# First step of a fused transformer block: x and weight loads take turns, and the first modulation product ends a step later

## The reference, cut to what matters

```python
# first block, first lines (l = 0)
x = x + 0.5 * swiglu(rms_norm(x, ffn1_norm[l]), ffn1_w_gate[l], ffn1_w_up[l], ffn1_w_down[l])
# swiglu(h, w_gate, w_up, w_down) = (silu(h @ w_gate) * (h @ w_up)) @ w_down
...
# second block: six vectors of 1024 out of one row c
c_act = silu(c)
mod = (c_act @ w_mod[l] + b_mod[l])[:, None, :]
```

## Time and profile before

| | |
|---|---|
| median of three executions | 1753.6 us (1753.0 to 1753.9) |
| profiled execution, own time | 1755.12 us |
| its span in the profile | 1753.2 us |
| PE busy | 1736.8 us, 99% |
| DVE, ACT, POOL busy | 1063.4, 738.9 and 197.1 us |
| the chain that ended last | PE 93%, DVE 3%, DMA 2%, ACT 1% |
| granted clock of PE, mean | 0.998 |

### The profile page before, as it was taken

The page is one execution under the profiler, slowest core; times in us unless marked ns, Lnnn a source line. Parts: engine busy times, 40 slices in busy tenths (PEclk is TensorE's granted clock), DMA queues, the critical chain, the costliest instruction groups (busy, mean ns, idle before and its releaser), DMA issues.

```text
span 1753.2 us, 23718 instructions
## 1 busy us (share of the span) xinstructions
PE 1736.8 (99%) x8898; PEld 1424.7 (81%) x8898; DVE 1063.4 (61%) x1649; ACT 738.9 (42%) x1043; POOL 197.1 (11%) x245
## 2 busy tenths in 40 slices
PE   8999999999999999999999999999999999999998
PEld 7888888888888777788888888888987888888887
DVE  6666537555563767655788853437588565555433
ACT  5322222333444887623333222225575455555321
POOL 2222001130000000004511020120004200000000
PEclk9999999999999999999999999999999999999999
DMA  7777422342222212123755552325132233222232
GB/s 246 249 226 226 138 75 81 107 151 96 97 73 96 73 49 69 55 94 111 220 180 157 147 169 81 99 90 187 47 144 73 73 104 98 99 98 83 81 102 78
DMA packets 171714, 206.87 MB, mean 118 GB/s; under 512 B 18420, under 2 KB 150130, under 8 KB 171122
## 3 DMA queue, kind: packets, MB, share of 16 engines
q1 hardware_dynamic: 145010, 161.97, 28.7%
q0 software_dynamic: 12640, 38.55, 7.0%
q10 hardware_dynamic: 13984, 5.27, 1.4%
HBM read 190.29 MB, written 17.56 MB: 119 GB/s over the span
## 4 chain that ended last, share of the span: by engine, by line
PE 93%; DVE 3%; DMA 2%; ACT 1%; issue 1%; SPq 0%; POOL 0%; DVEq 0%
PE bank L2270 40%; PE bank L2197 35%; PE bank L2548 5%; PE bank L2572 1%; PE bank L2669 1%; DMA w_raw<-in_w_in 1%; PE bank L2165 1%; PE bank L2288 1%; PE bank L2582 1%; PE bank L2923 1%; PE bank L2442 1%; PE bank L2935 1%; DMA w_raw<-in_ffn_w_gate 1%; PE bank L2791 0%; DMA mod_raw<-in_w_mod 0%
## 5 line engine op out<-in xcount | busy, mean ns | idle before, releaser
L737 ACT CAST w_hi<-w_raw 128x2048 fp32r<-128x2048 f32 x156 | 298.1, 1911 | 726.2 <-PE bank L2270 354.8
L1306 DVE TENSOR_TENSOR w_lo<-w_raw,w_hi 128x2048 fp32r<-128x2048 f32 x158 | 369.3, 2337 | 343.1 <-ACT w_hi L737 342.5
L2270 PE MATMUL bank<-h_hi,w_hi 128*128 128x512 f32 x1024 | 400.8, 391 | 0.5 <-DVE h_lo L1347 0.2
L2270 PE MATMUL bank<-h_hi,w_lo 128*128 128x512 f32 x1024 | 398.6, 389 | 0.0
L2270 PE MATMUL bank<-h_lo,w_hi 128*128 128x512 f32 x1024 | 315.4, 389 | 0.0
L2270 PEld LDWEIGHTS bank<-h_hi,w_hi 128*128 128x128 f32 x1024 | 192.2, 188 | 44.5 <-issue 3.2
L2270 PEld LDWEIGHTS bank<-h_lo,w_hi 128*128 128x128 f32 x1024 | 192.2, 188 | 40.2
L2270 PEld LDWEIGHTS bank<-h_hi,w_lo 128*128 128x128 f32 x1024 | 192.3, 188 | 39.2
L2197 PE MATMUL bank<-hid_hi,w_hi 128*128 128x512 f32 (+1 forms) x538 | 207.5, 386 | 0.0
L2197 PE MATMUL bank<-hid_lo,w_hi 128*128 128x512 f32 (+1 forms) x538 | 207.2, 385 | 0.0
L2197 PE MATMUL bank<-hid_hi,w_lo 128*128 128x512 f32 (+1 forms) x538 | 207.2, 385 | 0.0
(11 more groups left out here) (490 smaller groups left out, 2533.1 us busy)
## 6 DMA issues: line engine op xcount, KB each, us to landing
w_raw<-in_w_in SPq DMA_DIRECT2D x29, 1024.0 KB, 5.2
mod_raw<-in_w_mod POOLq DMA_DIRECT2D x96, 256.0 KB, 4.7
w_raw<-in_ffn_w_up SPq DMA_DIRECT2D x22, 1024.0 KB, 5.5
w_raw<-in_w_up SPq DMA_DIRECT2D x22, 1024.0 KB, 5.1
w_raw<-in_ffn_w_gate SPq DMA_DIRECT2D x21, 1024.0 KB, 6.4
w_raw<-in_ffn_w_down SPq DMA_DIRECT2D x16, 768.0 KB, 4.4
w_raw<-in_ffn_w_down SPq DMA_DIRECT2D x16, 640.0 KB, 3.9
w_raw<-in_w_out SPq DMA_DIRECT2D x8, 1024.0 KB, 5.2
```

The costliest lines, as they stand in the source:

```text
L737: act.copy(w_hi[i % 2][:], w_raw[i % 2][:]).then_inc(S("w_hi_done"), 1)
L1306: dve.tensor_tensor(w_lo[s][:], w_raw[s][:], w_hi[s][:].bitcast(F32), ALU.subtract).then_inc(S("w_split"), 1)
L2270: mm = pe.matmul(bank[:], w[:, k, at], h[:, k, :], start=k == first and part == 0 and i == 0, stop=k == last and part == 1)
```

## The change

SP now issues in this order: x tiles 0 and 1, the first half of panel 0, x tiles 2 and 3, the first half of panel 1, x tiles 4 to 7 in one load, the second half of panel 0, the second half of panel 1. PE has a first step of its own, in which transposes and products of half panels take turns; the six idle products behind the transposes are gone. ACT makes `h_hi` straight from the bank that the transpose wrote. DVE copies x from the bank after ACT has read it, and makes low parts of half panels; the first halves signal `w_lo_begun`, the second halves `w_split`. Modulation terms 0 to 3 of group 0 come ahead of the parameter copies, and terms 4 to 7 at the end of DVE's first step, behind `hid_lo`. PE's rows of group 0 stand in the second step, between its two panels. Group 1 moves on DVE from the start of the second step to behind the split of panel 4. Two semaphores (`ws_landed`, `c_landed`) become one.

```diff
-PHASES = {"ffn1": ((0, 1, True, None), (1, BESIDE_STEPS - 1, True, None), ...
+PHASES = {"ffn1": ((0, 1, True, None), (1, 2, True, None), (2, BESIDE_STEPS - 1, True, None), ...
+        X_QUARTERS = ((0, 2), (2, 4), (4, KD))
+        def x_bank(k):
+            return B[k if k >= 4 else 2 + k]
...
+                    gate_panel, up_panel = (panel(w_raw, i, KD, PC) for i in range(2))
+                    early, late = slice(0, KD // 2), slice(KD // 2, KD)
+                    load_x(0)
+                    sp.dma_start(gate_panel[:, early], gate_v[:, early, 0:PC]).then_inc(S("w0_tables_landed"), 16)
+                    load_x(1)
+                    sp.dma_start(up_panel[:, early], up_v[:, early, up_col:up_col + PC]).then_inc(S("first_up_landed"), 16)
+                    load_x(2)
+                    sp.dma_start(gate_panel[:, late], gate_v[:, late, 0:PC]).then_inc(S("w_landed0"), 16)
+                    sp.dma_start(up_panel[:, late], up_v[:, late, up_col:up_col + PC]).then_inc(S("w_landed1"), 16)
                     first = 1
                     load_parameters()
                     load(2, gate_v[:, :, PC:2 * PC], KD, PC)
...
 # ACT
+            first_hi((0, 1))
             act.wait_ge(S("w0_tables_landed"), 16)
+            act.copy(w_hi[0][:, early], w_raw[0][:, early]).then_inc(S("w0_begun"), 1)
+            first_hi((2, 3))
+            act.wait_ge(S("first_up_landed"), 16)
+            act.copy(w_hi[1][:, early], w_raw[1][:, early]).then_inc(S("w0_begun"), 1)
             act.wait_ge(S("w_landed0"), 16)
+            act.copy(w_hi[0][:, late], w_raw[0][:, late]).then_inc(S("w_hi_done"), 1)
+            first_hi(range(4, KD))
+            act.wait_ge(S("w_landed1"), 16)
+            act.copy(w_hi[1][:, late], w_raw[1][:, late]).then_inc(S("w_hi_done"), 1)
...
 # DVE, one step of the loop
                         if start == 0:
-                            modulation(i + MOD_AT[name], i, range(MOD_SLOTS))
+                            if name == "ffn2":
+                                modulation(i + MOD_AT[name], i, range(MOD_SLOTS))
                             refined_root({"ffn1": "n1", "ffn2": "n2"}[name])
-                        elif mods:
+                        elif mods and (name, start) != ("ffn1", 1):
...
                         split(i * 2 + (base + 2), base)
-                        if start == 0 and name == "ffn1":
-                            modulation(i + MOD_AT[name], i, range(MOD_SLOTS, KD))
+                        if start == 1 and name == "ffn1":
+                            modulation(i + MOD_AT[name], i)
...
                         split(i * 2 + (base + 3), base + 1)
                         for t in range(2):
                             hid_lo_of(name, i, t, 2 + t)
+                        if start == 0 and name == "ffn1":
+                            modulation(i + MOD_AT[name], i, range(MOD_SLOTS, KD))
 # DVE, ahead of the loop
+            first_x((0, 1))
+            first_lo((0, 1))
+            dve.wait_ge(S("w0_begun"), 1)
+            low_part(0, early, "w_lo_begun")
+            first_x((2, 3))
+            first_lo((2, 3))
+            dve.wait_ge(S("w0_begun"), 2)
+            low_part(1, early, "w_lo_begun")
+            first_x(range(4, KD))
+            first_lo(range(4, KD))
+            for i in range(2):
+                dve.wait_ge(S("w_hi_done"), i + 1)
+                low_part(i, late, "w_split")
+            modulation(0, 0, range(MOD_SLOTS))
             dve.wait_ge(S("rows_t"), 3)
 # PE
+                turned_x((0, 1))
+                pe.wait_ge(S("w0_begun"), 1)
+                first_products(0, (0, 1), w_hi, h_hi, ready_hi)
+                turned_x((2, 3))
+                first_products(0, (0, 1), w_hi, h_lo, ready)
+                pe.wait_ge(S("w_lo_begun"), 1)
+                first_products(0, (0, 1), w_lo, h_hi, ready_hi)
+                first_products(0, (2, 3), w_hi, h_hi, ready_hi)
+                first_products(0, (2, 3), w_hi, h_lo, ready)
+                first_products(0, (2, 3), w_lo, h_hi, ready_hi)
+                pe.wait_ge(S("w0_begun"), 2)
+                pe.wait_ge(S("x_turned"), 3)
+                first_products(1, early, w_hi, h_hi, ready_hi)
+                turned_x(late)
+                first_products(1, early, w_hi, h_lo, ready)
+                pe.wait_ge(S("w_lo_begun"), 2)
+                first_products(1, early, w_lo, h_hi, ready_hi)
+                pe.wait_ge(S("w_hi_done"), 1)
+                first_products(0, late, w_hi, h_hi, ready_hi)
+                first_products(0, late, w_hi, h_lo, ready)
+                first_sums()
+                pe.wait_ge(S("w_split"), 1)
+                first_products(0, late, w_lo, h_hi, ready_hi)
+                pe.wait_ge(S("w_hi_done"), 2)
+                first_products(1, late, w_hi, h_hi, ready_hi)
+                first_products(1, late, w_hi, h_lo, ready)
+                pe.wait_ge(S("w_split"), 2)
+                first_products(1, late, w_lo, h_hi, ready_hi)
...
                             by_k(base + half, [B[2 * half], B[2 * half + 1]], h_hi, h_lo)
+                            if (name, start, half) == ("ffn1", 1, 0):
+                                modulation_rows(0, True, False)
                         if mods:
+                            modulation_rows(i, name == "ffn2" and start == 0, stop == MOD_STOP[name])
```

More of the change, by code:

```diff
@@ L2296, in first_gate, with turned_x @@
                             mm.then_inc(S("pe_done"), 2)
-                if h_name == "n1":
-                    between()
+            def turned_x(ks):
+                for k in ks:
+                    pe.wait_ge(S(f"x_landed{min(k // 2, 2)}"), 16)
+                    if k in (4, 5):
+                        pe.wait_ge(S("x_turned"), k)
+                    for b in range(TB):
+                        mm = pe.transpose(x_bank(k)[:, b * P:(b + 1) * P], x_in[:, b, k * P:(k + 1) * P], ident[:])
+                    mm.then_inc(S("x_t"), 1)
@@ new lines, in first_products @@
+            def first_products(half, ks, w, h, wait):
+                weights = panel(w, half, KD, PC)
+                for k in ks:
+                    wait("n1")(k)
+                    for t in range(2):
+                        mm = pe.matmul(B[2 * half + t][:], weights[:, k, t * P:(t + 1) * P], h[:, k, :], start=k == 0 and w is w_hi and h is h_hi,
+                                       stop=k == KD - 1 and w is w_lo)
+                        if k == KD - 1 and w is w_lo:
+                            mm.then_inc(S("pe_done"), 2)
@@ new lines, in first_ffn_step @@
+            def first_ffn_step():
+                early, late = range(KD // 2), range(KD // 2, KD)
+                turned_x((0, 1))
[26 more added lines that the diff above has]
+                first_products(1, late, w_lo, h_hi, ready_hi)
@@ L2300, in gate_up, with modulation_rows @@
             def gate_up(name, h_name, free, sums=None):
                 base = BASE[name]
+                def modulation_rows(step, first, last):
+                    pe.wait_ge(S("mod_step"), step * MOD_STEPS + ((MOD_AT[name] + 1) * MOD_STEPS + MOD_SLOTS))
+                    for j in range(4):
+                        mm = pe.matmul(B[6][32 * j:32 * j + 32, 0:P], row_of[:], mod_acc[:, j * P:(j + 1) * P], start=first, stop=last)
+                    mm.then_inc(S("mod_acc_free"), 1)
                 for start, stop, mods, extra in PHASES.get(name, ((1, GU_STEPS, False, None),)):
+                    if name == "ffn1" and start == 0:
+                        first_ffn_step()
+                        continue
@@ L2424, in swiglu_free @@
                 return free
-            gate_up("ffn1", "n1", swiglu_free("ffn1"), first_sums)
+            gate_up("ffn1", "n1", swiglu_free("ffn1"))
             down("ffn1")
```

73 lines of the change are left out of this document (26 added, 47 removed).

## The result

The changed kernel takes 1767.42 us (median of six runs, 1766.53 to 1769.45), the kernel before 1753.8 on the same chip (1753.0 to 1755.28). The ratio is 1.0078, 95% interval 1.0065 to 1.0091: slower by 13.6 us, where I had forecast 6.6 and a range that ended at 1765.5. The profiled execution took 1767.36 us with a span of 1765.6, 12.4 more than the span before.

A forecast was written before the change was run, and what follows sets the result against it. PE holds 93% of the chain, so only time without products could pay. Late panel 3 moves step 3 from 61.43 to 68.05, +6.6 us: 1753.6 + 6.6 = 1760.2 us, range 1752.4 to 1765.5.

The forecast's parts named there:

- rival B: More is late: panel 3's 15.8 us repeats (landing 48.9), 1763.1; with clock falling before first products, 1765; chance 0.18.
- signs of being wrong: Panel 3 landing before 41 or group 0 rows ready; step 2 after 38 from DVE's lateness; clock 0.5 before 20 us.
- step 2 begins: End of PE's first step: products from 9.05, transposes, products and first sums end at 36.7 us instead of 39.02.
- PE's wait at the rows of group 0: Between PE's two panels of step 2: it arrives at 47.7 and waits L - 39.1, 6.9 us.
- step 3 begins: After group 1's rows: 46.0 + 21.6 + 0.45 = 68.05 us, before at 61.43, so +6.6.
- in the stretches read at the start it is 1.00: PE's granted clock in the kernel before's early stretches; the forecast charged no clock loss to the first products.
- L: Landing time of panel 3: 46.0 us taken, bounds 38.5 to 48.9, forecast's own range 43.5 to 48.5.
- the slow stretch: Transfers slowed around the spread loads ahead of panel 3: moves by 3.3 us, ends near 37 instead of 32 to 34.
- the rule of the Trainium skill: DMA engines alternate between queues packet by packet: panel 3 gets half the bandwidth, lands at 44.2, whole 1758.4 us.
- group 1 "just fits": Second modulation group, behind panel 4's split: terms end at L + 21, PE comes at L + 21.6; upper end 1.5 more.
- all later work hangs on signals of these engines and shifts with it: Everything behind step 3 shifts by the same +6.6 us, with nothing absorbed.
- the first step's own gain: Earlier products let step 2 begin at 36.7 rather than 39.02; less 0.4 for moved modulation rows, about 1.9 us remain.

The follow-up runs named there:

- Experiment 1: Changed kernel plus seven idle products between the transposes of x tiles 0 and 1 and the first product: 1761.44 us, ratio 1.0049.
- 7: Changed kernel plus seven idle products ahead of the first product, with the spread loads issued behind panel 5: 1757.88 us, ratio 1.0021.
- 9: Changed kernel plus seven idle products ahead of the first product, all spread loads behind the gate and up panel loop: 1754.93 us, ratio 1.0007.
- experiment 10: Changed kernel plus seven idle products, spread loads behind the panel loop, modulation terms of groups 0 and 1 split around the late panel's split: 1750.72 us, ratio 0.9988.
- experiment 8: Kernel before with one edit, the spread loads issued behind panel 5: 1753.70 us, ratio 0.9998.
- 2: Changed kernel with modulation terms 4 to 7 ahead of the split of panel 3 instead of behind `hid_lo`: 1763.52 us, ratio 1.0056.
- 3: Changed kernel with all spread loads issued behind panel 3 instead of ahead of it: 1762.27 us, ratio 1.0053.
- 4: Changed kernel with only the three element by element spread loads issued behind panel 3: 1762.09 us, ratio 1.0053.
- 11: Changed kernel plus seven idle products, spread loads behind the panel loop, modulation placed as in the kernel before: 1755.59 us, ratio 1.0014.
- 6: Changed kernel with the modulation and PE's rows of group 0 placed as in the kernel before: 1763.9 us, ratio 1.0055.

## Why the prediction was wrong in size

The direction and the mechanism were the ones forecast: panel 3 late, terms 4 to 7 behind it, PE idle at the rows of group 0. Of the two conditions of rival B (chance 0.18) both came true, a landing at about 48.9 and the fall of the clock ahead of the first products, and 1765 was its figure. Two of the signs of being wrong appeared: a clock of 0.5 before 20 us, and a step 2 behind 38, though not for the reason given there. By its terms:

| term | predicted | measured |
|---|---|---|
| first product | 9.05 | 8.28 |
| step 2 begins | 36.7 | 38.30 |
| panel 2 issued, landed | 25.4, 30.8 | 27.14, 32.5 |
| panel 3 issued, landed | 33.1, 46.0 | 34.00, 49.5 |
| PE's wait at the rows of group 0 | 6.9 | 8.8 |
| 48 products behind that wait | 11.0 + 1.5 | 12.69 |
| step 3 begins | 68.05 | 71.96 |
| behind it | +0 | +1.9 |

The step that failed is "in the stretches read at the start it is 1.00": I read the clock of a start in which idle products filled the gaps, and carried it to one in which they are gone, leaving the fall to rival B. Experiment 1 puts a price on it: 2.1 us at step 2, not 1.5, since the clock stays at half until about 14.5, and 2.8 of the 3.9 us by which step 3 was missed. The same experiment shows that the other terms of the first step were near: with the clock kept, step 2 begins at 36.24, panel 2 is issued at 25.07 and panel 3 at 31.94.

The second term is the landing of panel 3, mis-sized rather than misread: L was 49.5, 3.5 above the value taken and 0.6 above my upper bound of 48.9, which was reckoned from an issue at 33.1. Most of this is the clock again. I had the slow stretch end near 37; with the clock kept it lies at 30.5 to 37 and L is 46.9, and in the changed kernel, where panel 2 was issued 2.1 us later, it ends at 40. The rest is that from its end to the landing I took 9 us, where it was 9.9 and 9.5. From issue to landing panel 3's 15.5 us are nearly the 15.8 of the earlier trace rows over again, 14.95 with the clock kept, and I had taken 12.9. With the rule of the Trainium skill that I weighed (DMA: Bandwidth & Descriptors, Queues, rings and completion order) it would have been 44.2, further off; even from the measured end of the slow stretch at 40 its sum gives 47.2 against 49.5. No trace here counts the turns, so this speaks against my use of the rule, and neither for nor against the rule.

That a sum with L = 49.5 gives a step 3 at 71.6 (L + 22.05) against 71.96 measured shows that the remainder of the reckoning carried: the queue behind the wait, group 1 just in time, clock cost included. That group 1 "just fits" was right in the changed kernel only because PE was so late; in experiments 7 and 9 its rows are waited for, 6.7 and 2.5 us, once the first wait is gone.

The third is what lies behind step 3, which the sum put at nothing, because "all later work hangs on signals of these engines and shifts with it". It did shift unchanged as far as 1023 us; behind that the stop near 1300 with the fall behind it (3.6 us), less the fall at 1386 that stayed away (about 1.6), made it +1.9 between the spans. The 10.5 us lost up to step 3 would by themselves have given about 1764.3, within the range; it is this term that led out of it. Why PE stops there stays open. Finally, the first step's own gain, which I put at 1.9 us, is real (58.80 at step 3 in experiment 10 against 60.56 in experiment 8, both without spread loads near: 1.8) and was lost entirely in what it moved.

## What to carry to other kernels

An instruction moved on one engine moves all that its signal releases on the others: here the earlier start of PE issued two panels of the next steps later, since the signal that frees SP's queue now came behind more work. Look for small loads in the queue ahead of the transfer that is needed next, and put them where nothing with a due time is beside or behind them. When a wait is taken away, undo the next late thing in the same experiment, or the gain won't show: experiments 2, 3 and 7 removed the wait they were aimed at, 4 shortened it, and each met another; only number 10, which takes away the clock's fall, the spread loads and the order of terms at once, reached the gain. And read the clock of a gap only from a start that has that gap.

## What was not expected of the hardware

- The loads of `load_spread` (thirteen, together some 280 KB) hold all transfers together at 4 to 68 GB/s for seven to eight microseconds in the changed kernel, and at 13 to 52 for seven in the kernel before. With all or three of them behind panel 3, or all behind panel 5, the stretch lasts three to five and a half (3, 4 and 7). Without them nearby (9 to 11) there is no such stretch while panel 3 is under way. Transfers of another queue are held up with them: POOL's loads of terms 4 to 7 of group 0 take 8.5 to 9.2 us beside them and 3.1 to 5.5 with them moved away (7 and 9 to 11). The Trainium skill (DMA: Bandwidth & Descriptors, Why small descriptors are slow) counts the overhead of a 256 byte descriptor at about a quarter, which wouldn't make this stretch; eight of the loads are 32 KB spread over 128 partitions, so 256 bytes each. With the three element by element loads put behind panel 3 (4) the stretch of 8 to 37 GB/s is five microseconds instead of eight, so they have a part in it, and what the ten loads of rows would do without them wasn't tried.
- The granted clock of PE fell to 0.50 for some 6.8 us (8 to 14 us whole, and parts of the stretches beside) after a gap of only 1.85 us at the start (6.4 to 8.28 us), with transposes ahead of it, and seven idle products in that gap prevented it.
- Around 1386 us the same wait of 1.6 us is in all thirteen profiles; the clock fell behind it in three of them (before, 2 and 6) and was kept in the others. Each fall lasted 1.2 to 3.4 us, and the one in the kernel before costs about 1.6.
- Near 1300 us PE stops for 2.2 to 2.5 us in five kernels, with nothing in the profile that it waits for, and the clock falls behind the stop; together they cost 3.6 us in the changed kernel.
